# A norm factor on all 512 columns: sums by a matrix of ones, root and reciprocal wide

## The reference

```python
def _rmsnorm_2(x, g):
    x32 = x.astype(jnp.float32)
    y = x32 * lax.rsqrt(jnp.mean(x32 * x32, axis=-1, keepdims=True) + RMS_EPS)
    return (y * g.astype(jnp.float32)).astype(x.dtype)
...
for l in range(DEPTH_2):
    g = norm_g[l]
    f = _swiglu(_rmsnorm_2(x, g[0]), ffn_w_gate[l, 0], ffn_w_up[l, 0], ffn_w_down[l, 0])
    x = x + 0.5 * _rmsnorm_2(f, g[1])
    m = _mixer(_rmsnorm_2(x, g[2]), w_in[l], conv_w[l], pool_w[l], pool_scale[l], w_out[l])
    x = x + _rmsnorm_2(m, g[3])
    f = _swiglu(_rmsnorm_2(x, g[4]), ffn_w_gate[l, 1], ffn_w_up[l, 1], ffn_w_down[l, 1])
    x = x + 0.5 * _rmsnorm_2(f, g[5])
```

## Time and profile before

| | |
|---|---|
| median of 3 runs | 2501.86 us (2501.25 to 2501.88) |
| the profiled execution, its own time | 2502.55 us |
| span of its profile | 2500.8 us |
| mean granted TensorE clock | 0.996 |
| busy: PE, DVE, POOL, ACT | 99%, 48%, 43%, 37% |
| chain that ended last: PE, issue, DVE, POOL, ACT | 82%, 9%, 5%, 2%, 0% |

### The profile page before, as it was taken

The page is one execution under the profiler, slowest core; times in us unless marked ns, Lnnn a source line. Parts: engine busy times, 40 slices in busy tenths (PEclk is TensorE's granted clock), DMA queues, the critical chain, the costliest instruction groups (busy, mean ns, idle before and its releaser), DMA issues.

```text
span 2500.8 us, 33177 instructions
## 1 busy us (share of the span) xinstructions
PE 2480.0 (99%) x11581; PEld 2020.8 (81%) x11581; DVE 1191.7 (48%) x1748; ACT 924.7 (37%) x1315; POOL 1074.5 (43%) x508
## 2 busy tenths in 40 slices
PE   8999999999999999999999999999999999999999
PEld 5777888888888888778888888888888777888887
DVE  7664866254331345677431345331345677431332
ACT  3444443235322234544321234321234554431332
POOL 5332454445444444334443445444445334444444
PEclk9999999999999999999999999999999999999999
DMA  6223643322233232222233232233231322232232
GB/s 249 87 73 97 224 176 118 110 93 75 92 108 102 93 111 62 89 77 92 76 102 108 92 105 71 84 105 105 96 105 60 101 76 93 68 108 85 100 105 80
DMA packets 74060, 253.44 MB, mean 101 GB/s; under 512 B 9184, under 2 KB 13408, under 8 KB 73856
## 3 DMA queue, kind: packets, MB, share of 16 engines
q1 hardware_dynamic: 73984, 252.46, 30.5%
HBM read 244.76 MB, written 2.10 MB: 99 GB/s over the span
## 4 chain that ended last, share of the span: by engine, by line
PE 82%; issue 9%; DVE 5%; POOL 2%; ACT 0%; DMA 0%; DVEq 0%; SPq 0%; POOLq 0%; ACTq 0%
PE unit_bank L633 25%; PE unit_bank L634 25%; PE unit_bank L635 25%; POOL w_lo L510 2%; PE score L716 2%; DVE arena L2121 1%; PE score L706 1%; PE mix L683 1%; PE mix L852 1%; PE out_bank L832 1%; DVE x L2205 1%; DVE unit_bank L2203 1%; PE out_bank L688 1%; PE mix L860 0%; PE mix L930 0%
## 5 line engine op out<-in xcount | busy, mean ns | idle before, releaser
L510 POOL TENSOR_TENSOR w_lo<-raw,w_hi 128x1024 fp32r<-128x1024 f32 (+2 forms) x374 | 954.2, 2551 | 1303.5 <-ACT w_hi L1196 1303.5
L1196 ACT ACTIVATE w_hi<-raw 128x1024 fp32r<-128x1024 f32 (+2 forms) x375 | 416.2, 1110 | 1196.5 <-PE unit_bank L635 1172.2
L633 PE MATMUL unit_bank<-u_hi,w_hi 128*128 128x512 f32 x2152 | 843.1, 392 | 1.0 <-POOL w_lo L510 1.0
L635 PE MATMUL unit_bank<-u_hi,w_lo 128*128 128x512 f32 x2152 | 837.9, 389 | 0.0
L634 PE MATMUL unit_bank<-u_lo,w_hi 128*128 128x512 f32 x2152 | 837.7, 389 | 0.0
L633 PEld LDWEIGHTS unit_bank<-u_hi,w_hi 128*128 128x128 f32 x2152 | 404.0, 188 | 100.9 <-issue 14.3
L635 PEld LDWEIGHTS unit_bank<-u_hi,w_lo 128*128 128x128 f32 x2152 | 404.0, 188 | 84.4
L634 PEld LDWEIGHTS unit_bank<-u_lo,w_hi 128*128 128x128 f32 x2152 | 404.1, 188 | 82.8 <-issue 0.2
L633 PE MATMUL unit_bank<-h_hi,w_hi 128*128 128x512 f32 x981 | 382.7, 390 | 0.2 <-DVE h_lo L2045 0.2
L635 PE MATMUL unit_bank<-h_hi,w_lo 128*128 128x512 f32 x981 | 381.7, 389 | 0.0
L634 PE MATMUL unit_bank<-h_lo,w_hi 128*128 128x512 f32 x981 | 381.7, 389 | 0.0
(11 more groups left out here) (383 smaller groups left out, 2117.9 us busy)
## 6 DMA issues: line engine op xcount, KB each, us to landing
raw<-in_w_gate_up SPq DMA_DIRECT2D x168, 512.0 KB, 3.4
raw<-in_w_down SPq DMA_DIRECT2D x64, 704.0 KB, 4.1
raw<-in_w_in SPq DMA_DIRECT2D x65, 512.0 KB, 3.5
raw<-in_w_up SPq DMA_DIRECT2D x30, 512.0 KB, 3.5
f<-in_w_ada_rows SPq DMA_DIRECT2D x26, 512.0 KB, 5.2
raw<-in_w_out SPq DMA_DIRECT2D x24, 512.0 KB, 3.6
raw<-in_w_down SPq DMA_DIRECT2D x16, 512.0 KB, 3.4
ada_in_u<-in_w_ada SPq DMA_DIRECT2D x8, 512.0 KB, 11.5
```

What stands on the lines that cost most here:

```text
L510: e.tensor_tensor(w_lo[:, s, 0:n], raw[:, s, 0:n], as32(w_hi[:, s, 0:n]), ALU.subtract).then_inc(lo_ready, 1)
L633: e.matmul(bank[:], wh, hi(k), start=n == 0, stop=False)
L635: mm = e.matmul(bank[:], wl, hi(k), start=False, stop=last)
L1196: e.activation(w_hi[:, s, 0:n], raw[:, s, 0:n], ACT.Copy).then_inc(hi_ready, 1)
```

## The change

The factor that scales f is made wide from the start. TensorE multiplies a full 128 x 128 matrix of ones with `f_acc` and, when the last chunk is squared, with `f_sq`, both into `stat_bank`: each of the 128 partitions then holds the sum of squares of all 512 tokens. ScalarE takes the root of these 512 columns in place, VectorE the reciprocal in place, and the updates read it there. The first `spread` is gone, and so are five of the six `keep_warm` around the sums. The sums as 4 columns are still made (`token_sums`), since the next norm's factor needs `inv_f`; their reciprocal moves behind the update of chunk 0. VectorE's last addition to `gf_acc`, which stood behind the small reciprocal, now stands before the wide one.

```diff
@@ the matrix engine's norm(r)
                 token_sums(square_sum, f_acc, last=False)
-                keep_warm(3)
+                e.matmul(stat_bank[:], tab("ones"), f_acc, start=True, stop=False)
+                keep_warm(1)
                 e.wait_ge(fsq_ready, 2 * DC * r + 2 * (DC - 1) + 1)
+                e.matmul(stat_bank[:], tab("ones"), f_sq, start=False, stop=True).then_inc(sums_ready, 1)
                 token_sums(square_sum, f_sq, first=False).then_inc(sums_ready, 1)
-                keep_warm(3)
-                spread(2 * r + 1, inv_f, stat_bank)
-
@@ the scalar engine's norm(r, p, part, g)
-                e.wait_ge(sums_ready, r + 1)
+                e.wait_ge(sums_ready, 2 * r + 1)
+                e.activation(stat_bank[:], stat_bank[:], ACT.Sqrt, bias=eps[:], scale=1.0 / D).then_inc(rows_root, 1)
+                e.wait_ge(sums_ready, 2 * r + 2)
                 token_root(root_f, square_sum)
...
-                e.wait_ge(spread_ready, 2 * r + 2)
+                e.wait_ge(spread_ready, r + 1)
@@ the vector engine's norm(r, p, take, part, g, update)
                 chunk(p, 1, DC - 1, 1)
-                e.wait_ge(root_ready, 2 * r + 1)
-                e.reciprocal(inv_f, root_f).then_inc(inverse_ready, 1)
                 add_gf(DC - 1, gf_acc)
                 e.sem_inc(cross_ready, 1)
-                e.wait_ge(spread_ready, 2 * r + 1)
+                e.wait_ge(rows_root, r + 1)
+                step(e.reciprocal(stat_bank[:], stat_bank[:]))
                 for c in range(DC):
                     update(c)
+                    if c == 0:
+                        e.wait_ge(root_ready, 2 * r + 1)
+                        e.reciprocal(inv_f, root_f).then_inc(inverse_ready, 1)
                     if c == 3:
 
+                        e.wait_ge(inverse_ready, 2 * r + 1)
                         e.wait_ge(cross_sums, r + 1)
```

More of the change, by code:

```diff
@@ L265, in program @@
         fsq_added = sem("fsq_added")
+        rows_root = sem("rows_root")
         ux_ready = sem("ux_ready")
```

## The result

The changed kernel takes 2519.55 us (median of 6 runs, 2517.48 to 2520.05) against 2501.56 us (6 runs, 2497.65 to 2504.22): a ratio of 1.007, with an interval of 1.0059 to 1.0081. The profiled execution has a span of 2517.5 us against 2500.8. One execution of each kernel was profiled, and executions of one kernel differ: those of the kernel before lie between 2496.52 and 2506.28 us over all runs, with mean granted clocks from 0.998 down to 0.994. So what a single norm shows of the clock is one sample.

What follows compares the result with a forecast made beforehand. TensorE, 99% busy, was taken as the bound, with time lost in its waits. Norm 0 2.7, norms 1, 3, 4 8.7, norm 5 2.4, norm 2 0, clock 1.5: 15.3 us on 2502.55, forecast 2517, range 2510 to 2525.

Steps and rivals of the forecast that it cites:

- Sums by ones: In each norm's first piece, the wide ones-matrix products let the root start 3.22 us after the part's end, against 2.92.
- Wide root: ScalarE's root over 512 columns in each norm takes 0.67 us, against 0.26 for 4 columns.
- Wide reciprocal: VectorE's reciprocal over 512 columns in each norm takes 3.35 us, extrapolated from narrow rows.
- The rival of the copy's pace: The 512-column reciprocal streams like a copy, about 0.69 us, giving 2499.7 us, no change; chance 6%.
- that of eight times its pace: The 512-column reciprocal takes 8.25 ns per column, 4.4 us, giving 2523 us; chance 10%.
- a clock that stays low for long in every norm: Five norms lose 2.7 us each in the second piece, as norm 2 did, giving 2529 us; chance 6%.
- First update: In norms 0, 1, 3 and 4 it starts 7.40 us after the part's end instead of 4.72, 2.7 us later.
- Small reciprocal behind chunk 0: Moved behind the first chunk's update on VectorE, it adds 0.2 us in norms 1, 3, 4 and 5, nothing in norm 0.
- Norm 5: At half clock its first update comes at 9.33 us against 7.16; with the small reciprocal 2.4 us lost.
- Norm 2: Later update covered because TensorE was already behind in the second piece: 0 us, between a 1.9 gain and a 2.7 loss.
- The clock in norms 0, 1, 3 and 4: Half clock at the next part's start costs about 1.1 us in norm 0, 0.1 to 0.2 in the others, together 1.5.
- The hole: TensorE idles 2.7 us between its fillers and the next part's first product, and the clock falls in most of these norms.

Runs made afterwards that it cites:

- the last run: Changed kernel with every norm root and reciprocal in one early-loaded ScalarE activation, plus keep_warm behind the second sums and before the wait in norms 2 and 5: 2492.21 us.

## Why the prediction was right

The forecast was 2517 us with a range of 2510 to 2525, and slower with 93%. Measured 2519.55.

- *Sums by ones*: root at 3.22 us after the part's end; measured 3.26.
- *Wide root*: 0.67 us; measured 0.66.
- *Wide reciprocal*: 3.35 us from the last four of eight columns; measured 3.366 (six rows, 3365 to 3367 ns), so (3366 - 178) / 508 = 6.28 ns per column. The rival of the copy's pace (0.7 us) and that of eight times its pace (4.4 us) are both out. So is a clock that stays low for long in every norm: no second piece grew by 2.7 us. The Trainium skill's repeat count of 8 ("VectorE: DVE Perf Modes", section "First, the fixed hardware budget") is not a pace of eight times the copy's: by the rows here it is about six times.
- *First update*: 7.40; measured 7.35, the same in norms 0, 1, 3 and 4. Taking out the reciprocal brought the time back to that of before, so this step is shown.
- *Small reciprocal behind chunk 0*: 0.2 us; the second update comes 1.49 us after the first instead of 1.39, so 0.1.
- *Norm 5*: 2.4; measured 2.07, since the first piece took 8.92 us instead of 9.33: the forecast had it at half clock throughout, and over the sums the clock was low only from 2132.3 to 2135.7. *Norm 2*: 0; measured -0.25. Its second piece fell from 18.06 to 15.74 us as argued.
- *The clock in norms 0, 1, 3 and 4*: this term was mis-sized. I gave 1.5 us. The second pieces grew by 1.76, 0.93, 0.74 and 0.94, which is 4.1 us after the small reciprocal's 0.1 in three of them. The step that failed is "two or three us at half clock", which was to put TensorE 1.0 to 1.5 us behind. The clock came back only at 620.2, 992.3, 1569.1 and 1941.2, that is 4.4 to 4.8 us after the next part's first product (615.82, 987.47, 1564.75, 1936.38). At half pace this makes TensorE an estimated 2.2 to 2.4 us late. In norm 0, where it waited only 0.41 us for `u_hi` before, nearly all of that counts. In norms 1, 3 and 4 an estimated 1.5 us of it is absorbed in TensorE's waits for `u_hi` (2.1 us in norm 1 before), as argued; 0.6 to 0.8 us are left, not 0.1 to 0.2, because there was more to absorb. With the hole filled, all four terms vanished.
- *The hole*: 2.7 us expected, 3.10 shown in norm 1, and the clock fell within it in every one of the four norms. The hole is a cause and not the only one: filled, the clock held there; closed by the faster stand-in for the reciprocal, it still fell, for half as long.

The other terms came out 1.1 us below their forecast together (0.3 in norm 5, 0.25 in norm 2, 0.3 by the small reciprocal, 0.2 by the first updates) and the clock term 2.6 above; that makes the 1.4 us between 15.3 and the profile's 16.7. The medians differ by a little more, 18.0 us.

One thing the prediction didn't price was wrong in the reasoning though it changed no number. I treated the five fillers as products that nobody needs and their removal as free. In the kernel before, taking them out costs about 12 us. The change got away with it, likely because wide products took their places. What exactly TensorE must do for the clock to hold is left open: one-column sums with single waits of 0.52 and 0.72 us were followed by a fall, so were fully busy stretches with fillers of either kind between such sums, and the same instructions after the same wait were followed by one sooner or later.

## What to carry to other kernels

Price an operation at its own width: a reciprocal that costs 0.18 us on 4 columns costs 3.37 on 512, and its slope can be read from the last of the narrow rows. Spreading a factor that was found on few columns took 1.25 us from the small reciprocal's end (976.77) to the first update (978.02), and is cheap beside that. The wide form lost with VectorE's reciprocal, drew level with both in one activation that had to load its table on the path, and won with that table loaded early. The last version makes the small roots in the same way too, and the narrow form with that activation was not run, so it isn't shown that the wide form is what wins. Before taking out fillers from a stretch of narrow products, measure that alone: here it cost more than the fillers' own time, 10 us and more of 2501.

## What the runs showed of the hardware

- VectorE's reciprocal in fp32 takes 3366 ns on 128 x 512 in PSUM, where a multiply-and-add in place takes 700. ScalarE's Abs_reciprocal_sqrt takes 662 ns, exactly what its Sqrt takes.
- A table load ahead of an activation that waits for a semaphore starts before that wait ends (975.79, with the activation at 977.09 right behind it).
- Taking three 128-column fp32 products, 0.75 us of TensorE's time, from behind the second sums of each norm cost 0.40% of the kernel's time, and the mean granted clock of the profile fell from 0.996 to 0.989. The clock also fell from 0.96 to 0.53 behind a stretch in which TensorE was busy for 3.40 of 3.40 us (norm 3 of the last run).
- The clock fell 1.2 us after the first sums of norm 2 in one profile and 6.3 us after them in another, with the same instructions between and waits of 2.21 and 2.20 us ahead.
